# Stick-breaking scores as three products of high and low parts, with the low parts in two alternating sets of tiles

## The chip, the cores and the metric

The program runs on one core of a Trainium2 chip. The metric is the device time of one launch in microseconds. The kernel before took 2168.89 us (median of 3 runs, 2168.69 to 2169.61). In the profiles TensorE is PE (its weight loads PEld), VectorE is DVE, ScalarE is ACT, GpSimd is POOL and SyncE is SP.

## The reference, cut to what matters

A long chain of transformer blocks on 512 tokens of width 1024, float32 throughout. The part that the change touches is the stick-breaking attention, 16 heads of width 64:

```
qkv = (h @ w_qkv).reshape(b, s, 3, 16, 64)
z = einsum('bqhd,bshd->bhqs', q_blk, k) * 64**-0.5
causal = key_pos[None, :] < t[:, None]
log_1m = where(causal, log_sigmoid(-z), 0.0)
excl = cumsum(log_1m, axis=3, reverse=True) - log_1m
a = where(causal, exp(log_sigmoid(z) + excl), 0.0)
o = einsum('bhqs,bshd->bqhd', a, v)
```

A later block has another attention (two kinds of key sets, names nk_ks and nk_kw); it is not changed, but its scores are made in the way that the change brings to the stick-breaking ones.

## The kernel before

All activations lie transposed: features on the 128 partitions, the 512 tokens along the free axis. Large products are made from split operands: a high part rounded to fp32r and a low part (the rest), as hi*hi, hi*lo and lo*hi. ScalarE makes a high part (`act_hi`, `act_weights`), VectorE the low part from it (`dve_lo`, `dve_weights`), and TensorE takes three products of one pass each.

The stick-breaking stage (`pe_stick`, `act_stick`, `dve_stick`, `pool_stick`) works on head pairs c = 0 to 7: the two heads of a pair lie on partitions 0 to 63 and 64 to 127, and a pair's queries and keys are column blocks c of the tiles `q_s` and `k_s` (in the trace st_q and st_k). A pair takes four steps, n = 4c to 4c+3, for key blocks j = 3, 2, 1, 0, and the causal mask leaves 128, 256, 384 and 512 queries to them. In step n each engine works through its own written order, tied to the others by semaphores:

- TensorE: scores(n) into two PSUM banks (one per head), closed by a mask product of bf16 tiles (maskb, Ib); then the cumulative sums of step n-2 (`pe_stick_cum`, trir times high and low parts Lh, Ll); then half of a projection of queries or keys of the next pair (`pe_stick_qk`, 12 products of 512 columns); then the output product of step n-3 (`pe_stick_out`).
- VectorE: in every other step the low part of a weight unit (wl, L517) or, in the odd steps, the scaling of the finished projection out of PSUM into `q_s` (step 4c+1, L2615) or `k_s` (step 4c+3, L2617); then abs(n) (L2564), lo(n-1) (L2580), terms(n) (L2572), which waits for ScalarE's logarithm, and for two steps of four a low part of a sum (L2593). In steps 4c+2 it also splits a finished output (so_x, L571).
- ScalarE: the weights of step n-2 (exponential, L2515), in odd steps the high part of a weight unit (wh, L507), then exp(n) (L2530) and ln(n) (L2534); in steps 4 to 11 also the scaling of a block of the residual H (L2540).
- GpSimd: the high part of step n (L2689), sums of columns over key blocks (L2604, L2606, L2608), and in steps 4 to 11 the product of a block of H with rs1 (L2697).

The first two projections (pair 0) are made before the value projections, and the last head pair's keys are projected in steps 25 and 26; from step 27 on TensorE has no projection to fill a step with. Buffers are handed over by `plan` (who uses a buffer, and which marks free it) and `take` (waits for those marks). `NB` is the one PSUM bank in which projections land.

Of the kernel before, what the change touches and what calls it, by code (L numbers as in the profile page):

```python
# [4 lines left out]
F = mybir.dt.float32  # L5
# [201 lines left out]
def program(nc, A, cols_d, const_d, out_d):  # L207
# [85 lines left out]
    def plan(buf, ev, *freed):  # L293

        assert ev not in use, ev
        use[ev] = (buf.t, buf.freed)
        buf.freed = list(freed)
# [7 lines left out]
    def got(ev):  # L305
        return use[ev][0]
# [236 lines left out]
    def mm(e, out, a, b, start, stop):  # L543
        return e.matmul(out, a, b, start=start, stop=stop, skip_group_check=True)  # L544
# [68 lines left out]
    def plan_spread(n):  # L613
        plan(NB, ("spread", n), (a_made, ("rs", n)))
        plan(tmp.next(), ("diag", n), (mixed, ("spread", n)))
# [1661 lines left out]


    ph = Phase(XAT, "st")
    q_s = ph.sb("q", [128, 8, S])  # L2280
    k_s = ph.sb("k", [128, 8, S])
    XO = Pair(*(Phase(XAT + 4 * 8 * S * i, f"so{i}").sb("x", [128, 8, S], R) for i in range(2)))
    ph = Phase(PH0 + 32768, "st")
    v_s = ph.sb("v", [128, 4, D])
    rs1 = Phase(PH0 + 92160, "st").sb("rs1", [128, S])
    wd = [512 - 128 * j for j in range(4)]
    wl_ = [512, 384, 384, 128]
    ST = [(c, j) for c in range(8) for j in (3, 2, 1, 0)]
# [35 lines left out]
    OUT_LAST = [(2, 0, 3), (0, 7, 8), (1, 7, 8), (2, 3, 8)]  # L2324

    def plan_stick():
        for o in QK[0:2]:
            plan(psr.next(), ("sqk", o), (v_made, ("sqk", o)))
        for blk in range(2):
            token_plan(f"sv{blk}", 4)  # L2330
            if blk == 0:
                plan_spread("st")
        plan_spread("one")
        pairs = Ring([0, 1, 2])
        for n in range(-1, NST):
            u, half = next_qk(n)
            if u is not None and half == 0:
                plan(NB, ("sqk", QK[u]), (v_made, ("sqk", QK[u])))
            if n < 0:
                continue  # L2340
            c, j = ST[n]
            at = pairs.next()
            for m in range(2):
                plan(PS[2 * at + m], ("sk", n, m), (a_made, ("sw", n, m)))
            plan(Lp.next(), ("L", n), (mixed, ("so", n)))
            reader = [(scored, ("cum", n + 1 if j else n))]
            if j >= 2:
                reader.append((g_made, ("sum", n + 1)))
            plan(Lh[j].next(), ("Lh", n), *reader)
            plan(Ll[j].next(), ("Ll", n), *reader)  # L2350
            if j == 2:
                plan(sum2, ("sum", n), (v_made, ("lo_sum", n)))
            if j == 1:
                plan(sum1, ("sum", n), (v_made, ("lo_sum", n)))
                plan(later, ("later", n), (scored, ("cum", n + 1)))
            if j == 3:
                plan(PS[6], ("so", c), (x_lo, ("so", c)))
        for o, b in enumerate([NB, PS[4], PS[5], PS[0], PS[1], PS[2], PS[3], PS[6]]):
            plan(b, ("soo", o), (h_new, ("st", o)))
        plan_next("m")  # L2360
# [36 lines left out]
    def pe_stick_scores(e, n):  # L2397

        c, j = ST[n]
        e.wait_ge(*v_made.at("sqk", c))  # L2400
        e.wait_ge(*v_made.at("sqk", 8 + c))
        bk = [take(e, ("sk", n, m))[:, 0:wd[j]] for m in range(2)]
        for m in range(2):
            p0 = 64 * m
            mm(e, bk[m], k_s[p0:p0 + 64, c, 128 * j:128 * j + 128], q_s[p0:p0 + 64, c, 128 * j:512], True, False)
        for m in range(2):
            mm(e, bk[m][:, 0:128], Ib[:, :], maskb[:, 2, :], False, False).then_inc(*scored.up("z", n, m))

# [53 lines left out]
    def pe_stick(e):  # L2462
# [21 lines left out]
            project(e, f"so{o}", XO, "so", t[:, :], ("soo", o))  # L2484
        pe_.end("st")

    def act_stick(e):
        act_weights(e, UI["sv02"])
        fence(e, "f")
# [7 lines left out]
        for blk in range(2):  # L2497
            for c in range(4):
                act_weights(e, UI[f"sv{blk}{c}"] + 2)
                if blk == 0 and c == 2:  # L2500
                    act_rs(e, "st", [(v_made, ("f", ff.last_up))])
            if blk == 0:
                e.wait_ge(*v_made.at("inv", "st"))
            act_tokens(e, f"sv{blk}", lambda t: v_s[:, t, 512 * blk:512 * blk + 512], 512, 4, inv("st"))
# [12 lines left out]
        for n in range(-1, NST + 3):  # L2517
            if 2 <= n < NST + 2:
                weights_of(n - 2)
            u, half = next_qk(n)  # L2520
            if u is not None and half == 0:
                act_weights(e, UI[f"sq{QK[u]}"] + 2)
            if n == NST - 2:
                act_weights(e, UI["so2"])
            if 0 <= n < NST:
                c, j = ST[n]
                L = got(("L", n))
                for part in parts(n):
                    e.wait_ge(*v_made.at("abs", n, heads_of(part)[-1]))
                    e.activation(L[:, part, 0:wd[j]], L[:, part, 0:wd[j]], ACT.Exp, scale=-1.0).then_inc(  # L2530
                        *a_made.up("exp", n, part.start))
                for part in parts(n):
                    e.wait_ge(*a_made.at("exp", n, part.start))
                    e.activation(L[:, part, 0:wd[j]], L[:, part, 0:wd[j]], ACT.Ln, bias=ONE1).then_inc(  # L2534
                        *a_made.up("ln", n, part.start))
            if 4 <= n < 12:
                k = n - 4
                e.wait_ge(*h_new.at("f5", k))
                e.wait_ge(*x_lo.at("st", k))
                e.activation(H[:, k, :], H[:, k, :], ACT.Copy, scale=col("first", k)).then_inc(*a_made.up("first", k))  # L2540
            if n >= 6 and n % 4 == 2:
                c = n // 4 - 1
                e.wait_ge(*mixed.at("so", 4 * c + 3))
                act_hi(e, XO, "so", c, got(("so", c))[:, :])
# [63 lines left out]
        e.tensor_scalar(sum_parts(n)[0], f[:, :, :], 1.0, 0.0, ALU.mult, ALU.add).then_inc(*g_made.up("hi_sum", n))  # L2608

    def dve_stick_qk(e, o):  # L2610
        b, t = o % 8, got(("sqk", o))
        e.wait_ge(*proj.at("sqk", o))
        e.wait_ge(*a_made.at("rs", "st"))
        if o < 8:
            f = e.scalar_tensor_tensor(q_s[:, b, :], t[:, :], 0.125, rs[:, :], ALU.mult, ALU.mult)  # L2615
        else:
            f = e.tensor_tensor(k_s[:, b, :], t[:, :], rs[:, :], ALU.mult)  # L2617
        f.then_inc(*v_made.up("sqk", o))

    def dve_stick(e):  # L2620
        dve_weights(e, UI["sv02"])
# [13 lines left out]
        for blk in range(2):  # L2635
            for c in range(4):
                dve_weights(e, UI[f"sv{blk}{c}"] + 2)
                if blk == 0 and c == 2:
                    for o in QK[0:2]:
                        dve_stick_qk(e, o)  # L2640
        dve_diag(e, "one")
        for n in range(-1, NST + 3):
            u, half = next_qk(n)
# [7 lines left out]
                dve_stick_abs(e, n)  # L2651
            if 1 <= n < NST + 1:
                dve_stick_lo(e, n - 1)
            if 0 <= n < NST:
                dve_stick_terms(e, n)
            if 1 <= n < NST + 1 and ST[n - 1][1] in (1, 2):
# [963 lines left out]
```

## Time and profile before

| | |
|---|---|
| profiled execution, its own time | 2170.64 us |
| its span | 2168.8 us |
| median of 3 runs | 2168.89 us |
| PE busy | 2133.5 us (98%) |
| DVE, ACT, POOL busy | 71%, 46%, 34% |
| chain that ended last | PE 90%, DVE 4%, ACT 3% |
| stick-breaking steps, about | 906 to 1080 us of the span |

The profile is of one execution, somewhat longer than the median of the runs; a sum of changes is made against it and carried over to the median as a difference. A row's mean duration includes the time that an instruction is held up inside its engine, and on TensorE successive products overlap, so that what a group of products takes is read from start to start.

### The profile page before, as it was taken

To read this page: it belongs to the slowest core of one execution; us is meant where nothing else is said; L and a number is where in the kernel's file an instruction comes from. 1 tells how busy PE (TensorE), PEld (TensorE's weight loads), DVE (VectorE), ACT (ScalarE), POOL (GpSimd) and SP (SyncE) were. 2 spreads that over 40 slices of the span, in tenths; PEclk is the share of its full clock that TensorE was granted. 3 is DMA by queue.
4 is the path that set the end of the run, shared out by engine and by line. 5 is a ranking of instruction groups with operands and counts; after the bars stand their busy time and mean duration, and the time that the engine had idled before them with its cause. 6 is when DMAs were issued, how large, how long until landed. Compare 5 with 4: busy or idle time off the path is not lost.

```text
span 2168.8 us, 32272 instructions
## 1 busy us (share of the span) xinstructions
PE 2133.5 (98%) x12632; PEld 1776.1 (82%) x12632; DVE 1533.2 (71%) x2130; ACT 1003.7 (46%) x1690; POOL 728.4 (34%) x604
## 2 busy tenths in 40 slices
PE   8999999999999999999999999999989999999998
PEld 7888788888999998766688998988865568898987
DVE  5866566558988886386668777765567756877774
ACT  4433464445544444365554343344426755333434
POOL 2301330017434434164464232310136636332321
PEclk9999999999999999999999999999999999999999
DMA  5233125223333333311133323323410012323231
GB/s 177 83 107 88 50 78 170 74 59 88 98 117 98 117 96 89 88 49 49 30 88 99 116 88 107 115 80 123 121 49 2 1 38 80 117 82 114 89 106 49
DMA packets 292679, 188.06 MB, mean 87 GB/s; under 512 B 7856, under 2 KB 286768, under 8 KB 292528
## 3 DMA queue, kind: packets, MB, share of 16 engines
q1 hardware_dynamic: 292240, 185.78, 28.5%
q8 instruction: 101, 1.65, 0.3%
q14 instruction: 50, 0.41, 0.1%
q10 hardware_dynamic: 288, 0.21, 0.0%
HBM read 183.88 MB, written 2.10 MB: 86 GB/s over the span
## 4 chain that ended last, share of the span: by engine, by line
PE 90%; DVE 4%; ACT 3%; issue 2%; POOL 0%; DMA 0%; ACTq 0%; DVEq 0%; POOLq 0%
PE ps L544 88%; PE ps L578 2%; ACT wh L507 1%; DVE wl L517 1%; DVE H L687 0%; DVE tmp L1174 0%; ACT sq L621 0%; DVE tt_t L1921 0%; DMA p_xt<-in_x 0%; DVE sb_small L3228 0%; ACT tp_tb L1899 0%; DVE tp_up L2178 0%; ACT xb_x L565 0%; POOL acc L631 0%; DVE st_Ll L2580 0%
## 5 line engine op out<-in xcount | busy, mean ns | idle before, releaser
L517 DVE TENSOR_TENSOR wl<-raw,wh 128x1024 fp32r<-128x1024 f32 (+1 forms) x336 | 433.2, 1302 | 251.5 <-ACT wh L507 251.0
L544 PE MATMUL ps<-xb_x,wh 128*128 128x256 f32 (+1 forms) x1584 | 389.7, 337 | 1.9 <-DVE wl L517 0.7
L507 ACT CAST wh<-raw 128x1024 fp32r<-128x1024 f32 (+1 forms) x336 | 324.3, 980 | 137.6 <-PE ps L544 128.9
L544 PEld LDWEIGHTS ps<-xb_x,wh 128*128 128x128 f32 x1584 | 266.0, 188 | 32.6 <-issue 1.1
L544 PE MATMUL ps<-tt_t,wh 128*128 128x256 f32 x1536 | 277.8, 280 | 2.7 <-ACT tp_q L2105 2.6
L544 PE MATMUL ps<-xb_x,wl 128*128 128x256 f32 (+1 forms) x792 | 265.0, 335 | 0.0
L544 PEld LDWEIGHTS ps<-tt_t,wh 128*128 128x128 f32 x1536 | 237.5, 188 | 6.6 <-ACT tp_q L2105 3.6
L544 PE MATMUL ps<-XH,wh 128*128 128x512 f32 (+2 forms) x632 | 234.5, 371 | 4.3 <-issue 3.4
L544 PE MATMUL ps<-XH,wl 128*128 128x512 f32 (+2 forms) x632 | 229.6, 363 | 0.0
L544 PE MATMUL ps<-XL,wh 128*128 128x512 f32 (+2 forms) x632 | 229.3, 363 | 0.0
L544 PE MATMUL ps<-tt_t,wl 128*128 128x256 f32 x768 | 214.6, 279 | 0.0
L631 POOL TENSOR_TENSOR acc<-acc,sq 128x512 f32<-128x512 f32 x55 | 79.4, 1444 | 397.0 <-ACT sq L621 396.2
L529 POOL TENSOR_TENSOR su_s<-raw 128x512 f32<-128x512 f32 x48 | 65.1, 1356 | 397.3 <-DVE wl L517 376.6
L517 DVE TENSOR_TENSOR wl<-su_s,wh 128x1024 fp32r<-128x1024 f32 x96 | 124.1, 1293 | 57.1 <-ACT wh L507 56.7
L544 PEld LDWEIGHTS ps<-xb_x,wl 128*128 128x128 f32 x792 | 149.2, 188 | 16.3
L687 DVE TENSOR_TENSOR H<-H,ps 128x512 f32<-128x512 f32 x200 | 135.2, 679 | 23.6 <-PE ps L544 23.5
L544 PEld LDWEIGHTS ps<-tt_t,wl 128*128 128x128 f32 x768 | 144.7, 188 | 0.0
L544 PEld LDWEIGHTS ps<-XH,wh 128*128 128x128 f32 (+1 forms) x632 | 119.4, 189 | 24.8 <-issue 4.5
L544 PEld LDWEIGHTS ps<-XH,wl 128*128 128x128 f32 (+1 forms) x632 | 119.3, 189 | 19.5
L544 PEld LDWEIGHTS ps<-XL,wh 128*128 128x128 f32 (+1 forms) x632 | 119.5, 189 | 18.6 <-issue 0.7
L507 ACT CAST wh<-su_s 128x1024 fp32r<-128x1024 f32 x96 | 100.5, 1047 | 19.0 <-PE ps L544 16.6
L538 POOL TENSOR_TENSOR su_s<-raw,raw 128x512 f32<-128x512 f32 x48 | 70.3, 1464 | 103.8 <-DVE wl L517 103.8
(427 smaller groups left out, 4695.1 us busy)
## 6 DMA issues: line engine op xcount, KB each, us to landing
raw<-in_mlp_w SPq DMA_DIRECT2D x128, 512.0 KB, 4.0
raw<-in_w_gate_up SPq DMA_DIRECT2D x44, 512.0 KB, 4.0
raw<-in_w_in SPq DMA_DIRECT2D x29, 512.0 KB, 3.6
raw<-in_sb_w_qkv SPq DMA_DIRECT2D x24, 512.0 KB, 3.7
raw<-in_w_down SPq DMA_DIRECT2D x22, 512.0 KB, 5.9
raw<-in_w_out_mix SPq DMA_DIRECT2D x16, 512.0 KB, 3.7
raw<-in_w_kv SPq DMA_DIRECT2D x16, 512.0 KB, 4.0
raw<-in_nsa_w_kv SPq DMA_DIRECT2D x12, 512.0 KB, 3.7
```

Of the source, the lines that this page charges most:

```text
L507: e.copy(shaped(WH[i % NH], i), source(i)).then_inc(*w_hi.up(i))
L517: e.tensor_tensor(shaped(WL[i % NH], i), source(i), shaped(WH[i % NH], i).bitcast(F), ALU.subtract).then_inc(*w_lo.up(i))
L529: e.tensor_tensor(SU[0][:, 0:4, :], tb[:, 0::2, :], tb[:, 1::2, :], ALU.add).then_inc(*g_made.up())
L538: e.tensor_tensor(SU[1][:, 4:8, :], ta[:, 0::2, :], tb[:, 0::2, :], ALU.subtract).then_inc(*g_made.up())
L544: return e.matmul(out, a, b, start=start, stop=stop, skip_group_check=True)
L578: f = e.transpose(out[0:p, o:o + src.shape[0]], src, ident)
L631: e.tensor_tensor(a[:, :], a[:, :], got(("sq", n, k))[:, :], ALU.add).then_inc(*g_made.up("acc", n, k))
L687: e.tensor_tensor(H[:, o, :], H[:, o, :], src, ALU.add).then_inc(*h_new.up(ver, o))
```

## The change

Queries and keys of a head pair are no longer multiplied as float32 but as split operands. VectorE's scaling of a projection now writes a float32 tile (`tmp.bufs[2]` for queries, `tmp.bufs[3]` for keys); ScalarE rounds it into `q_s` or `k_s`, now fp32r (`act_stick_qk`); VectorE subtracts and writes the low part (`dve_stick_qk_lo`) into one of two sets of tiles, taken in turn by the pair's parity. The scores are k_hi*q_hi, k_hi*q_lo and k_lo*q_hi, each for both heads. The new waits: the first score product of a pair waits for the low parts of its queries and keys (`x_lo`), where it waited for the scaling; the low part waits for the high part; a float32 tile is free again when its low part is made, and a set of low tiles when the last scores of the pair two earlier are made.

```
+    q_s = ph.sb("q", [128, 8, S], R)
+    k_s = ph.sb("k", [128, 8, S], R)
...
+    phl = Phase(PH0 + 94208, "sl")
+    qk_lo = [[Phase(PH0 + 90112, "sl").sb("a", [128, S], R), phl.sb("b", [128, S], R)],
+             [phl.sb(f"c{i}", [128, S], R) for i in range(2)]]
+    qk_low = [[Buf(t) for t in pair] for pair in qk_lo]
...
+        def plan_parts(u):
+            o = QK[u]
+            plan(tmp.bufs[2 + u % 2], ("qkt", o), (x_lo, ("qk", o)))
+            plan(qk_low[o % 8 % 2][o // 8], ("qkl", o), (scored, ("z", 4 * (o % 8) + 3, 1)))
...
     def pe_stick_scores(e, n):
         c, j = ST[n]
-        e.wait_ge(*v_made.at("sqk", c))
-        e.wait_ge(*v_made.at("sqk", 8 + c))
+        e.wait_ge(*x_lo.at("qk", c))
+        e.wait_ge(*x_lo.at("qk", 8 + c))
         bk = [take(e, ("sk", n, m))[:, 0:wd[j]] for m in range(2)]
-        for m in range(2):
-            p0 = 64 * m
-            mm(e, bk[m], k_s[p0:p0 + 64, c, 128 * j:128 * j + 128], q_s[p0:p0 + 64, c, 128 * j:512], True, False)
+        ql, kl = got(("qkl", c)), got(("qkl", 8 + c))
+        for k, q, first in ((k_s[:, c, :], q_s[:, c, :], True), (k_s[:, c, :], ql, False),
+                            (kl, q_s[:, c, :], False)):
+            for m in range(2):
+                p = slice(64 * m, 64 * m + 64)
+                mm(e, bk[m], k[p, 128 * j:128 * j + 128], q[p, 128 * j:512], first, False)
...
+    def act_stick_qk(e, o):
+        e.wait_ge(*v_made.at("sqk", o))
+        e.copy((k_s if o >= 8 else q_s)[:, o % 8, :], got(("qkt", o))[:, :]).then_inc(*x_hi.up("qk", o))
...
     def act_stick(e):
+                if blk == 0 and c == 3:
+                    for o in QK[0:2]:
+                        act_stick_qk(e, o)
...
+            if half == 0 and 2 < (n + 1) // 2 + 2 <= 16:
+                act_stick_qk(e, QK[(n + 1) // 2 + 1])
             if 0 <= n < NST:
...
     def dve_stick_qk(e, o):
-            f = e.scalar_tensor_tensor(q_s[:, b, :], t[:, :], 0.125, rs[:, :], ALU.mult, ALU.mult)
+            f = e.scalar_tensor_tensor(d[:, :], t[:, :], 0.125, rs[:, :], ALU.mult, ALU.mult)
...
+    def dve_stick_qk_lo(e, o):
+        d, hi = take(e, ("qkl", o)), (k_s if o >= 8 else q_s)[:, o % 8, :]
+        e.wait_ge(*x_hi.at("qk", o))
+        e.tensor_tensor(d[:, :], got(("qkt", o))[:, :], hi.bitcast(F), ALU.subtract).then_inc(*x_lo.up("qk", o))
...
     def dve_stick(e):
+                if blk == 1 and c == 0:
+                    for o in QK[0:2]:
+                        dve_stick_qk_lo(e, o)
...
             if 1 <= n < NST + 1:
                 dve_stick_lo(e, n - 1)
+            if half == 0 and 2 < (n + 1) // 2 + 2 <= 16:
+                dve_stick_qk_lo(e, QK[(n + 1) // 2 + 1])
             if 0 <= n < NST:
                 dve_stick_terms(e, n)
```

Where the instructions stand now, on VectorE in the last step of a head pair (n = 4c+3). Names: so_x is the output of the pair before, st_L the work tile of a step, st_Lh and st_Ll its high and low part; tmp_78 is the new float32 tile of the keys, sl_b their low part. Line numbers are those of each kernel. Before:

```order
L571 TENSOR_TENSOR so_x<-ps,so_x 128x512
L2617 TENSOR_TENSOR st_k<-ps,rs 128x512
L2564 TENSOR_SCALAR st_L_144<-ps 128x512 x2
L2580 TENSOR_TENSOR st_Ll_151<-st_L_143,st_Lh_146 128x384 x2
L2572 SCALAR_TENSOR_TENSOR st_L_144<-ps,st_L_144 128x512 x2
L2593 TENSOR_TENSOR sr_l<-sr_f_157,sr_h 128x512
L517 TENSOR_TENSOR wl_66<-raw_56,wh_62 128x1024
```

Now:

```order
L571 TENSOR_TENSOR so_x<-ps,so_x 128x512
L2645 TENSOR_TENSOR tmp_78<-ps,rs 128x512
L2592 TENSOR_SCALAR st_L_148<-ps 128x512 x2
L2608 TENSOR_TENSOR st_Ll_155<-st_L_147,st_Lh_150 128x384 x2
L2651 TENSOR_TENSOR sl_b<-tmp_78,st_k 128x512
L2600 SCALAR_TENSOR_TENSOR st_L_148<-ps,st_L_148 128x512 x2
L2621 TENSOR_TENSOR sr_l<-sr_f_161,sr_h 128x512
L517 TENSOR_TENSOR wl_66<-raw_56,wh_62 128x1024
```

The low part of the keys stands behind abs and both halves of lo(n-1), and ahead of terms(n).

On ScalarE in the same step, with the waits of each instruction. Before:

```order
L563 CAST so_x<-ps 128x512 [waits mixed]
L2515 ACTIVATE st_L_142<-ps 128x256 [waits scored,pool_made]
L2515 ACTIVATE st_L_142<-ps 128x256 [waits scored]
L507 CAST wh_64<-raw_59 128x1024 [waits projected,weights_in_3]
L2530 ACTIVATE st_L_144<-st_L_144 128x512 [waits dve_made] x2
L2534 ACTIVATE st_L_144<-st_L_144,small 128x512 [waits act_made] x2
```

Now:

```order
L563 CAST so_x<-ps 128x512 [waits mixed]
L2541 ACTIVATE st_L_146<-ps 128x256 [waits scored,pool_made]
L2541 ACTIVATE st_L_146<-ps 128x256 [waits scored]
L507 CAST wh_64<-raw_59 128x1024 [waits projected,weights_in_3]
L2508 CAST st_k<-tmp_78 128x512 [waits dve_made]
L2558 ACTIVATE st_L_148<-st_L_148 128x512 [waits dve_made] x2
L2562 ACTIVATE st_L_148<-st_L_148,small 128x512 [waits act_made] x2
```

The rounding of the keys stands between the weight unit and exp(n); in step 4c+1 that of the queries stands at the same place.

On TensorE where the next pair begins, before:

```order
L544 MATMUL ps<-st_L_141,st_v 64x128 x2
L544 MATMUL ps<-st_q,st_k 128x128 [waits act_made]
L544 MATMUL ps<-st_q,st_k 128x128
L544 MATMUL ps<-maskb,Ib 128x128 x2
L544 MATMUL ps<-st_Lh_146,trir 128x384 [waits dve_made]
```

Now (sl_c_143 and sl_c_144 are the low parts of that pair's queries and keys):

```order
L544 MATMUL ps<-st_L_145,st_v 64x128 x2
L544 MATMUL ps<-st_q,st_k 128x128 [waits act_made,x_lo]
L544 MATMUL ps<-st_q,st_k 128x128
L544 MATMUL ps<-sl_c_143,st_k 128x128 x2
L544 MATMUL ps<-st_q,sl_c_144 128x128 x2
L544 MATMUL ps<-maskb,Ib 128x128 x2
L544 MATMUL ps<-st_Lh_150,trir 128x384 [waits dve_made]
```

The first product of the pair now waits for x_lo, and the two float32 products have become six.

## Rows read from the trace of the kernel before

**Rows 1.** Page of the profile, part 4: shares of the chain that ended last, by engine
```profile
PE 90%; DVE 4%; ACT 3%; issue 2%; POOL 0%; DMA 0%; ACTq 0%; DVEq 0%; POOLq 0%
```

**Rows 2.** Busy time by stretch: stretch, its length, each engine's busy us (instructions), PEclk, DMA share, GB/s
```profile
945.60:967.85 22.25, 22.25 (x122) 15.23 (x120) 18.76 (x30) 14.72 (x28) 16.48 (x17) 1.00 0.16 48
```

**Rows 3.** Timeline of TensorE, scores today: start us, us, engine, line, operation, tiles, count
```profile
967.85 0.49 PE L544 MATMUL ps<-st_q,st_k 64*128 64x128 f32 x4
973.06 0.70 PE L544 MATMUL ps<-st_q,st_k 64*128 64x256 f32 x4
979.37 0.92 PE L544 MATMUL ps<-st_q,st_k 64*128 64x384 f32 x4
984.71 1.13 PE L544 MATMUL ps<-st_q,st_k 64*128 64x512 f32 x4
985.77 0.28 PE L544 MATMUL ps<-maskb,Ib 128*128 128x128 bf16 x2
```

**Rows 4.** Timeline of TensorE, scores of the later attention, made as three products
```profile
1662.71 0.50 PE L544 MATMUL ps<-nk_kwh,xb_x 64*128 64x512 f32 x2
1663.61 0.29 PE L544 MATMUL ps<-maskb,Ib 128*128 128x128 bf16 x2
1665.72 0.45 PE L544 MATMUL ps<-nk_kwh,xb_x 64*128 64x384 f32 x2
1666.44 0.28 PE L544 MATMUL ps<-maskb,Ib 128*128 128x128 bf16 x2
1668.11 0.39 PE L544 MATMUL ps<-nk_kwh,xb_x 64*128 64x256 f32 x2
1668.67 0.29 PE L544 MATMUL ps<-maskb,Ib 128*128 128x128 bf16 x2
1669.91 0.33 PE L544 MATMUL ps<-nk_kwh,xb_x 64*128 64x128 f32 x2
1670.39 0.29 PE L544 MATMUL ps<-maskb,Ib 128*128 128x128 bf16 x2
```

**Rows 5.** Timeline of VectorE around the change to head pair 3
```profile
963.18 0.69 DVE L571 TENSOR_TENSOR so_x<-ps,so_x 128x512 fp32r<-128x512 f32 x1 [0.42 <-ACT so_x L563]
965.58 2.00 DVE L2580 TENSOR_TENSOR st_Ll<-st_L,st_Lh 128x384 fp32r<-128x384 f32 x2
967.77 1.30 DVE L2572 SCALAR_TENSOR_TENSOR st_L<-ps,st_L 128x512 f32<-128x512 f32 x2 [0.19 <-ACT st_L L2534]
```

**Rows 6.** Timeline of GpSimd, same stretch
```profile
964.97 1.30 POOL L2606 TENSOR_TENSOR sr_f<-sr_f,st_Ll 128x512 f32<-128x512 f32 x1
966.36 0.82 POOL L2608 TENSOR_SCALAR sr_h<-sr_f 128x512 fp32r<-128x512 f32 x1
967.14 1.58 POOL L2697 TENSOR_TENSOR H<-H,st_rs 128x512 f32<-128x512 f32 x1
```

**Rows 7.** Timeline of VectorE, the other head pairs and the end
```profile
920.48 2.22 DVE L2580 TENSOR_TENSOR st_Ll<-st_L,st_Lh 128x384 fp32r<-128x384 f32 x2
978.77 0.76 DVE L2572 SCALAR_TENSOR_TENSOR st_L<-ps,st_L 128x256 f32<-128x256 f32 x2 [3.06 <-ACT st_L L2534]
987.84 1.02 DVE L2580 TENSOR_TENSOR st_Ll<-st_L,st_Lh 128x384 fp32r<-128x384 f32 x2
1054.59 1.02 DVE L2580 TENSOR_TENSOR st_Ll<-st_L,st_Lh 128x384 fp32r<-128x384 f32 x2
1055.99 1.30 DVE L2572 SCALAR_TENSOR_TENSOR st_L<-ps,st_L 128x512 f32<-128x512 f32 x2 [0.38 <-ACT st_L L2534]
```

**Rows 8.** Timeline of ScalarE, same change as rows 5
```profile
965.03 1.04 ACT L507 CAST wh<-raw 128x1024 fp32r<-128x1024 f32 x1
```

**Rows 9.** Groups by line and form, ScalarE: busy us, mean ns, idle before
```profile
L563 ACT CAST fm_h<-tp_up 128x512 fp32r<-128x512 f32 x32 | 19.9, 621 | 111.4 <-DVE tp_up L2178 111.4
```

**Rows 10.** Timeline of TensorE at the end of the stage
```profile
1054.28 0.49 PE L544 MATMUL ps<-st_q,st_k 64*128 64x128 f32 x4 [0.20 <-ACT st_L L2515]
1058.99 0.50 PE L544 MATMUL ps<-st_Lh,trir 128*128 128x512 f32 x1 [0.60 <-DVE st_Ll L2580]
```

More of the change, by code:

```diff
@@ L2279, in program @@
     ph = Phase(XAT, "st")
-    q_s = ph.sb("q", [128, 8, S])
-    k_s = ph.sb("k", [128, 8, S])
+    q_s = ph.sb("q", [128, 8, S], R)
+    k_s = ph.sb("k", [128, 8, S], R)
     XO = Pair(*(Phase(XAT + 4 * 8 * S * i, f"so{i}").sb("x", [128, 8, S], R) for i in range(2)))
@@ L2326, in plan_stick, with plan_qk @@
     def plan_stick():
+        def plan_qk(o, bank):
+            plan(bank, ("sqk", o), (v_made, ("sqk", o)))
+        def plan_parts(u):
+            o = QK[u]
+            plan(tmp.bufs[2 + u % 2], ("qkt", o), (x_lo, ("qk", o)))
+            plan(qk_low[o % 8 % 2][o // 8], ("qkl", o), (scored, ("z", 4 * (o % 8) + 3, 1)))
         for o in QK[0:2]:
-            plan(psr.next(), ("sqk", o), (v_made, ("sqk", o)))
+            plan_qk(o, psr.next())
         for blk in range(2):
@@ L2332, in plan_stick @@
                 plan_spread("st")
+        for u in range(2):
+            plan_parts(u)
         plan_spread("one")
+        for u in range(2, 16):
+            plan_parts(u)
         pairs = Ring([0, 1, 2])
@@ L2337, in plan_stick @@
             if u is not None and half == 0:
-                plan(NB, ("sqk", QK[u]), (v_made, ("sqk", QK[u])))
+                plan_qk(QK[u], NB)
             if n < 0:
@@ L2610, in dve_stick_qk @@
     def dve_stick_qk(e, o):
-        b, t = o % 8, got(("sqk", o))
+        d, t = take(e, ("qkt", o)), got(("sqk", o))
         e.wait_ge(*proj.at("sqk", o))
@@ L2614, in dve_stick_qk @@
         if o < 8:
-            f = e.scalar_tensor_tensor(q_s[:, b, :], t[:, :], 0.125, rs[:, :], ALU.mult, ALU.mult)
+            f = e.scalar_tensor_tensor(d[:, :], t[:, :], 0.125, rs[:, :], ALU.mult, ALU.mult)
         else:
-            f = e.tensor_tensor(k_s[:, b, :], t[:, :], rs[:, :], ALU.mult)
+            f = e.tensor_tensor(d[:, :], t[:, :], rs[:, :], ALU.mult)
         f.then_inc(*v_made.up("sqk", o))
+    def dve_stick_qk_lo(e, o):
+        d, hi = take(e, ("qkl", o)), (k_s if o >= 8 else q_s)[:, o % 8, :]
+        e.wait_ge(*x_hi.at("qk", o))
+        e.tensor_tensor(d[:, :], got(("qkt", o))[:, :], hi.bitcast(F), ALU.subtract).then_inc(*x_lo.up("qk", o))
     def dve_stick(e):
```

## The prediction

> **What bounds the kernel now.** The page of the profile comes first: the chain that ended last is PE for 90% [rows 1]. A change in one stage has to be read from that stage, so next the busy time by stretch: a head pair of the stick-breaking stage takes 22.25 us, in which PE is busy for all 22.25, DVE for 18.8, ACT for 14.7, POOL for 16.5, at full clock [rows 2]. The scores of pairs 1 to 6 start at 923.36, 945.60, 967.85, 990.10, 1012.35 and 1034.60, one period apart (945.60 and 967.85 are the ends of rows 2): nothing makes PE wait there. What PE saves there counts one for one, if DVE and ACT, which get more to do, deliver in time. In the last pair PE does wait (two waits are in rows 10), and there VectorE and ScalarE set the pace.
>
> **What PE gains.** The scores of one step now take, from their first product to the next group, 0.43, 0.63, 0.85 and 1.06 us for 128, 256, 384 and 512 queries. Rows 3 show 1.06 for the widest (984.71 to 985.77); the row says 1.13, so a row overlaps the next by 0.07, and the others, 0.49, 0.70 and 0.92, give 0.42, 0.63 and 0.85. Sum of a pair: 2.96 us. The new form is in the trace already, in the later attention: three products of high and low parts, two heads on 64 partitions each, the same weights' width, the same kind of products ahead and the same mask behind [rows 4]. There the group takes 1663.61-1662.71 = 0.90, 0.72, 0.56 and 0.48, sum 2.66. The gain is 0.16, 0.13 and 0.07 for the wide ones and a loss of 0.06 for the narrowest, 0.30 us a pair. The two heads run side by side there: six times 512 columns one after the other, a column a cycle at the full clock of 2.4 GHz, would be 1.28 us, and the group takes 0.90. So the gain is small from the start: 8 x 0.30 = 2.4 us at most.
>
> **What is added beside it.** Sixteen roundings on ACT and sixteen subtractions on DVE. A rounding of 128x512 from a float32 tile takes 0.62 us [rows 9]; successive instructions overlap a little, and I take 0.55 as the shift of what follows. A subtraction of 128x512 I take at 0.68: two of 128x384 take 1.02 when undisturbed (at 987.84 in [rows 7]), 0.51 each, times 4/3. The pair 0 ones lie in the value projections, where PE has only large products; no product waits for them (uncovered they would cost 0.55 + 0.68 each). The queries' subtraction (step 4c+1) lies before terms(n), where DVE waits 3.06 us for ACT (at 978.77) [rows 7]: hidden; without that idle time it would push DVE back by 0.68. The queries' rounding delays exp, ln and terms of step 4c+1 by 0.55, and with them GpSimd, which from there works without a gap to the end of the next two steps. Instruction counts on PE grow by 4 products a step; their time is in the 0.90.
>
> **The keys' subtraction is not hidden.** It stands in step 4c+3 behind lo(n-1), and PE's next group of scores waits for it; behind that group PE's queue holds the sums of step n-1, half a projection and an output product, and ACT and DVE wait for the first two. So the question is when lo(n-1) ends and when PE comes. Work it out for the change to pair 3. PE comes at 967.85 [rows 3], or, since the products of the two steps after the last common point (PE's output product, which so_x waits for) shrink by 0.13 and 0.16, at 967.56. lo ends at 965.58+2.00 = 967.58 [rows 5]. Already with the bare 0.68 behind it the low part would be 0.7 us late.
> It gets later, for DVE and POOL hinder each other. The two halves of lo take 2.00 us here and 1.02 at 987.84. The first starts at 965.58 while POOL's L2606 runs till 966.27; then POOL's L2608 shows 0.82 us and ends at 967.18, and DVE's second half ends 0.40 after that; then POOL's L2697, issued at 967.14, ends 1.14 after DVE is done [rows 5, 6]. The rows read as strict turns between DVE instructions with two SBUF inputs and POOL's. With turns: POOL comes 0.55 later by the queries' rounding, so L2606 ends at 966.8, DVE's first half at 967.25, L2608 at 967.7, the second half at 968.1, and L2697, which has been waiting longer than the keys' subtraction, at 969.3; the subtraction behind it ends at 969.85. PE starts 2.3 us late. The Trainium skill, page "SBUF — State Buffer", section "Summary: rules for kernel authors", says that where DVE has two SBUF inputs and GpSimd reads SBUF, the second to issue "fully blocks until the first finishes". By that rule the wait is the 2.3 us; if the two only slowed each other, so that the subtraction ran from 967.6 at the doubled 1.0 us, it would be about 1.0.
> L2697 exists in steps 4 to 11 only, so the 2.3 us fall due twice, at the changes to pairs 2 and 3: 4.6 us.
> Change to pair 1 (923.36): lo is 920.48+2.22 = 922.70 [rows 7], with no L2697 behind it; the subtraction ends at 923.35, PE comes at 923.05 (three wide groups and a narrow one saved 0.30): wait 0.3.
> Changes to pairs 4, 5, 6: lo ends at 988.86, one turn later with POOL's shift 989.1, the subtraction 989.75; PE comes at 990.10-0.29 = 989.81. Wait 0, and with little to spare; bounds 0 and 0.4 each.
> Change to pair 7: PE has no projection in step 27 and comes at 1054.28 [rows 10], the subtraction ends behind lo (1054.59+1.02 = 1055.61 [rows 7]) at about 1056.4, 2.1 us later, but here DVE and ACT set the pace and PE has idle time of its own. The rounding pushes terms(27) from 1055.99 [rows 7] to about 1056.4, and PE, with scores, sums and scores in front of it, reaches the sums of step 27 perhaps 0.6 later than 1058.99 [rows 10]; one group's gain of 0.1 goes off. I take +0.5; the bounds are 0 and the whole 2.1.
> ACT's shift of 0.55 in step 4c+3 lies beside DVE's: ACT's weight cast ends at 966.07 [rows 8], the rounding at 966.6, so the high part is there before lo ends. terms(n), now at 967.77 [rows 5], follow the subtraction, but PE needs them only in its sums of step n+2, six us later, and is itself late by then.
>
> **The sum.** Gain 0.30-0.31 for six pairs that are bounded by PE: -1.8 to -1.9. Waits: 0.3 + 4.6 + 0. End: +0.5. Net +3.5 us. Against the profiled execution's own time, 2170.64 us (span 2168.8 and 1.8 around it), this is 2174.1; against the median of the runs, 2168.89, which stands 1.75 lower, 2172.4. That is 0.16%. About 0.2%, or 4.3 us, is what a measurement of this kernel can tell from no change.
>
> **The rivals.**
> A, DVE keeps up: the low parts never stop PE, because so_x and all behind it on DVE follow PE's faster steps or POOL lets DVE through. 2168.9-2.4 = 2166.5. For it speaks only DVE's idle share; against it that lo ends at 967.58 when PE wants to start at 967.56. Chance 0.08.
> B, contention without turns: the subtraction passes ahead of L2697; waits of 1.0 to 1.25 at two changes: net +1.0 to +1.4, 2170.1. Chance 0.22.
> C, the slower one: every one of the seven changes makes PE wait, because the place of the keys' subtraction has no room at the changes to pairs 4 to 6 either (0.06 us spare by my sum), and at those with L2697 a further POOL instruction gets in between. It decides from 0.1 us more on DVE or POOL. Three waits of 0.4 and 0.7 more at each of the two: 3.5+1.2+1.4 = +6.1, 2175.0. Chance 0.23.
> D, the products don't behave as in the later attention: the bounds are the two heads one after the other (3 x 1280 more columns a pair, 1.6 us, 13 us in all, 2185) and no overhead beside the columns (1.0 us a pair off, 8 us in all, 2164). Nothing in the rows speaks for either: chance 0.04, half each side.
> The forecast has 0.43.
>
> **How the numbers follow.** Forecast 2172.4, its own range 2171.2 to 2173.6. The range leaves out A and D and most of C's upper end: 2168.6 to 2175.6. Faster by over 0.2% (under 2164.6) is left to D's lucky half and to what I don't see: 0.04. Slower by over 0.2% (over 2173.2) are C, D's other half and the upper edge of the forecast, 0.23+0.02+0.05: 0.30. Within: 0.66.
>
> **What the changed profile would show.** Score groups of 0.48, 0.56, 0.72 and 0.90 us start to start. PE idle just ahead of the first scores of a pair, released by DVE's subtraction (tile sl): about 2.3 us at pairs 2 and 3, 0.3 at pair 1, none or little at 4 to 6, about 2 at 7. At pairs 2 and 3 the subtraction should show 1.8 us, ending right after POOL's L2697 plus 0.6. Periods of 24.2 us for the pairs with L2697 and 21.95 for the later ones. I am wrong in the mechanism if PE never waits on sl, or waits alike everywhere; wrong in size if the subtraction overtakes L2697; wrong in the place if the time sits outside 900 to 1080 us.

## The result, and the profile after

| kernel | median us (lowest to highest, runs) | to the kernel before |
|---|---|---|
| before | 2168.81 (2168.69 to 2169.61, 4) | |
| changed | 2176.99 (2176.27 to 2178.76, 4) | 1.0038 [1.0026, 1.0050] |

The change costs 8.2 us, 0.38%. I had said 2172.4, 2168.6 to 2175.6: slower than I had it, and outside the range. A second measurement of the same kernel (`after2`) gave 2177.87, 1.0041 [1.0029, 1.0054]. The profiled execution of the changed kernel took 2178.76 (span 2176.6), the slowest of its four; the profiled execution of `after2` is the median one of its five (2177.87, span 2175.8), and sums are made with it.

The chain is still TensorE's, with a little more of VectorE in it. Page of the changed kernel, part 4 (answers to [rows 1]):

```profile
PE 89%; DVE 5%; ACT 3%; issue 2%; POOL 0%; DMA 0%; ACTq 0%; DVEq 0%; POOLq 0%
```

Busy time by stretch, changed kernel: a head pair with GpSimd's product of H in it, and a later one (columns as in [rows 2]):

```profile
945.68:971.46 25.78, 23.83 (x128) 17.21 (x128) 21.04 (x32) 15.86 (x29) 16.47 (x16) 0.93 0.15 41
993.59:1015.73 22.14, 22.14 (x130) 15.86 (x129) 17.40 (x31) 13.43 (x26) 10.27 (x12) 1.00 0.16 48
```

Before, both took 22.25. The later pair is only 0.11 shorter, although the scores in it are 0.30 shorter; the earlier one is 3.5 longer, and two things show in its row: PE is idle for 1.95 of it, and its granted clock is 0.93.

What PE waits for in the stage, 900 to 1095 us, without the one wait at its start (0.7 us for st_rs) that both kernels have (engine, tile, line waited for: us in total, times, longest). Changed kernel:

```profile
PE ps L544 <- DVE sl_c L2651: 4.8, 3, 2.8
PE ps L544 <- DVE sl_b L2651: 1.9, 1, 1.9
PE ps L544 <- DVE st_Ll L2608: 1.8, 2, 1.1
```

Kernel before:

```profile
PE ps L544 <- DVE st_Ll L2580: 2.3, 4, 0.9
PE ps L544 <- ACT st_L L2515: 0.5, 2, 0.3
```

The subtraction (L2651) is the new releaser, 6.7 us of it; each of these waits stands at the first scores of a pair. Timeline of TensorE in the changed kernel, those first scores (pairs 1, 2, 3, 5, 7) and the widest group of pair 4:

```profile
921.49 0.33 PE L544 MATMUL ps<-st_q,st_k 64*128 64x128 f32 x2 [0.16 <-DVE sl_c L2651]
945.68 0.33 PE L544 MATMUL ps<-st_q,st_k 64*128 64x128 f32 x2 [1.90 <-DVE sl_b L2651]
971.46 0.33 PE L544 MATMUL ps<-st_q,st_k 64*128 64x128 f32 x2 [1.85 <-DVE sl_c L2651]
1010.30 0.50 PE L544 MATMUL ps<-st_q,st_k 64*128 64x512 f32 x2
1011.19 0.29 PE L544 MATMUL ps<-maskb,Ib 128*128 128x128 bf16 x2
1015.73 0.33 PE L544 MATMUL ps<-st_q,st_k 64*128 64x128 f32 x2
1059.82 0.47 PE L544 MATMUL ps<-st_q,st_k 64*128 64x128 f32 x2 [2.76 <-DVE sl_c L2651]
```

The widest group takes 1011.19-1010.30 = 0.89, the narrowest 0.48, the others 0.55 and 0.73, as in [rows 4] within 0.01. Note 0.47 at 1059.82 where the same row says 0.33 elsewhere.

Around the change to pair 3 (answers to [rows 5] and [rows 6]), VectorE and then GpSimd:

```profile
967.25 2.49 DVE L2608 TENSOR_TENSOR st_Ll<-st_L,st_Lh 128x384 fp32r<-128x384 f32 x2
969.66 1.75 DVE L2651 TENSOR_TENSOR sl_c<-tmp,st_k 128x512 fp32r<-128x512 f32 x1
971.33 1.27 DVE L2600 SCALAR_TENSOR_TENSOR st_L<-ps,st_L 128x512 f32<-128x512 f32 x2
```

```profile
968.52 0.81 POOL L2636 TENSOR_SCALAR sr_h<-sr_f 128x512 fp32r<-128x512 f32 x1
969.30 1.56 POOL L2735 TENSOR_TENSOR H<-H,st_rs 128x512 f32<-128x512 f32 x1
```

The subtraction is issued at 969.66, the product of H (issued before it, at 969.30) ends at 970.86, the subtraction 0.55 after that, and PE starts at 971.46. At pair 5, with no product of H, it runs undisturbed:

```profile
1013.43 1.43 DVE L2608 TENSOR_TENSOR st_Ll<-st_L,st_Lh 128x384 fp32r<-128x384 f32 x2
1014.78 0.68 DVE L2651 TENSOR_TENSOR sl_c<-tmp,st_k 128x512 fp32r<-128x512 f32 x1
```

1.75 against 0.68: the turns are there. The rule I had weighed (the Trainium skill, "SBUF — State Buffer", "Summary: rules for kernel authors") fits this.

The clock is what I had left out. Busy time by stretch, changed kernel, behind the waits of pairs 2, 3 and 7 (the third column from the right is the granted clock of TensorE):

```profile
947.00:950.00 3.00, 3.00 (x11) 2.61 (x10) 3.00 (x5) 1.49 (x4) 3.00 (x2) 0.50 0.00 0
974.00:978.00 4.00, 4.00 (x26) 2.75 (x24) 4.00 (x8) 0.93 (x2) 2.36 (x2) 1.00 0.44 131
1060.00:1066.00 6.00, 6.00 (x30) 4.58 (x31) 4.09 (x11) 1.79 (x4) 2.04 (x3) 0.50 0.00 0
```

TensorE had been idle for 1.90 us ahead of the first, 1.85 ahead of the second and 2.76 ahead of the third, and after the first and third it works at the lower of its two levels, 1.2 GHz instead of 2.4, on the products that everything waits for. In `after2` pair 2 is at full clock (1.00 over 947 to 950 us), and pair 7 is at half for most of the stretch (0.55 over 1060 to 1066). In the kernel before no stretch of the stage is below 1.00.

**The sum, read off two profiles** (before and `after2`; first scores of a step to first scores of another). The first scores of step 27, the last of pair 6, and of step 31, the last of the stage, are these, in the kernel before:

```profile
1051.45 1.13 PE L544 MATMUL ps<-st_q,st_k 64*128 64x512 f32 x4
1065.82 1.13 PE L544 MATMUL ps<-st_q,st_k 64*128 64x512 f32 x4
```

and in `after2`:

```profile
1053.58 0.50 PE L544 MATMUL ps<-st_q,st_k 64*128 64x512 f32 x2
1071.56 0.50 PE L544 MATMUL ps<-st_q,st_k 64*128 64x512 f32 x2
```

From pair 0 to the last step of pair 6 145.11 us became 148.53, +3.42. From there to the last scores of the stage 14.37 became 17.98, +3.61. From those scores to the end 1103.02 became 1104.21, +1.19; in 1600 to 1660 us, which the change doesn't touch, the granted clock is 0.94 in the one and 0.89 in the other. Together +8.22. (The spans differ by 6.9 only, since the profile of before has half clock near 540 us, 0.91 over 530 to 550 us where `after2` has 1.00, and with it reaches the stage at 906.34 instead of 905.05.)

### The profile page after: what moved, and what is told of

It is laid out like the page before. It is cut to its first block, busy times and chain, and to the rows that moved or that the text cites. A ratio compares the mean times of both kernels' runs of the same rounds, so it can differ in the third digit from the quotient of the medians.

```text
span 2176.6 us, 32447 instructions
## 1 busy us (share of the span) xinstructions
PE 2135.2 (98%) x12696; PEld 1782.6 (82%) x12696; DVE 1549.2 (71%) x2146; ACT 1012.5 (47%) x1706; POOL 729.5 (34%) x604
## 4 chain that ended last, share of the span: by engine, by line
PE 89%; DVE 5%; ACT 3%; issue 2%; POOL 0%; DMA 0%; ACTq 0%; DVEq 0%; POOLq 0%
PE ps L544 87%; PE ps L578 2%; ACT wh L507 1%; DVE wl L517 1%; DVE st_Ll L2608 0%; DVE st_L L2592 0%; DVE H L687 0%; DVE tmp L1174 0%; ACT sq L621 0%; ACT XH L565 0%; ACT p_xscr L727 0%; DMA p_xt<-in_x 0%; ACT st_L L2558 0%; DVE st_L L2600 0%; ACT tp_tb L1899 0%
```

## The experiments

Twelve kernels in three groups (the first four rows, the next four, the last four), each group on a chip of its own with the kernel before beside it (2168.81, 2168.95 and 2169.35); across groups the ratios are what to compare. T is the theory of the prediction, that the low parts come late through their place and through the turns with GpSimd; the expectations add to it the half clock behind the waits, which the prediction did not have.

| kernel | median us | ratio [interval] |
|---|---|---|
| `after2`, the changed kernel | 2177.87 | 1.0041 [1.0029, 1.0054] |
| `load` | 2171.71 | 1.0012 [1.0003, 1.0021] |
| `nolow` | 2169.05 | 1.0000 [0.9992, 1.0009] |
| `filler` | 2174.42 | 1.0025 [1.0015, 1.0034] |
| `fe` | 2171.56 | 1.0011 [1.0002, 1.0020] |
| `early` | 2171.86 | 1.0012 [1.0003, 1.0021] |
| `early_fe` | 2169.34 | 1.0001 [0.9993, 1.0010] |
| `before_fe` (control) | 2170.27 | 1.0003 [0.9994, 1.0012] |
| `nb` | 2174.33 | 1.0025 [1.0014, 1.0037] |
| `best` | 2167.79 | 0.9992 [0.9984, 1.0001] |
| `best_nofe` | 2168.50 | 0.9997 [0.9988, 1.0006] |
| `before_nb` (control) | 2169.59 | 0.9999 [0.9991, 1.0008] |

**after2.** No edit.

> The changed kernel as it is, once more, as the measure for the others. Theory T: the 8 us are (1) the wait of TensorE for the keys' low part at the seven changes of head pair, about 6 us in sum, and (2) TensorE running at half its clock after the waits of 1.9 us and more (change to pairs 2, 3 or 7), about 1.6 us after pair 2 and some 3 us around pair 7, less (3) the gain of some 2 us in the products. Then this run lies at 2176.3 to 2178.8 again, and where a long wait is not followed by half clock it lies lower. Rival L (load): the sixteen roundings and subtractions slow the stage by themselves, wherever they stand. Rival P (products): the three products cost more than they save.

Measured 2177.87 (2176.03 to 2180.27). Its profile has the waits at the same places; the half clock at pair 2 is missing. The mean granted clock of an execution goes with its time: 0.991 at 2180.27, 0.992 at 2177.87, 0.994 at 2176.03. So the scatter between executions is at least partly the clock's.

**load: the added instructions alone.** The kernel before, with roundings and subtractions made into spare tiles that nobody reads.

```
+        e.copy(xh_[u % 2][:, :], (k_s if o >= 8 else q_s)[:, o % 8, :]).then_inc(*x_hi.up("qk", o))
...
+        e.tensor_tensor(xl_[u % 2][:, :], (k_s if o >= 8 else q_s)[:, o % 8, :], xh_[u % 2][:, :].bitcast(F), ALU.subtract).then_inc(*x_lo.up("qk", o))
```

> The kernel before with the change's roundings and subtractions added at the change's places, but with scores still float32 and TensorE not waiting for the low parts (they are made and not used). T: TensorE idles nowhere before pair 7, nothing falls to half clock; 2168.8 to 2170.2 (+0 to +1.4, all of it in the last pair). L: this kernel bears the same load, so it is as slow as the changed one or slower: 2175 or more.

2171.71, between the two. What PE waits for on VectorE in `load`, and of its two longest waits the one in pair 2:

```profile
PE ps L544 <- DVE st_Ll L2595: 4.4, 6, 0.9
```

```profile
951.42 0.51 PE L544 MATMUL ps<-st_Lh,trir 128*128 128x512 f32 x1 [0.95 <-DVE st_Ll L2595]
```

Nobody waits for the spare tile, but it still costs 2.9 us: VectorE, held back by the subtraction in step 7 (1.78 us beside GpSimd), delivers lo(7) late for the sums of that step, which PE makes in step 9, and the same again four steps on, in the two pairs with GpSimd's product of H (1.17 and 1.13 us more from the scores of step 4c+1 to the next). The other 0.6 lies in the last pair. In the changed kernel this does not come on top: PE has already lost more than that at the first scores, and the same step takes 6.20 to 6.23 us there, undisturbed. So neither theory's number came out. The load has a price of its own, and in the changed kernel it is contained in the wait ahead of it.

**nolow: everything but the subtraction.** All pairs use the low parts of pair 0 in place of their own (so the scores of pairs 1 to 7 are not the reference's); 14 subtractions are gone, the products and roundings stay, and the first scores of a pair wait for the rounding instead.

```
-        ql, kl = got(("qkl", c)), got(("qkl", 8 + c))
+        ql, kl = got(("qkl", 0)), got(("qkl", 8))
...
-            if half == 0 and 2 < (n + 1) // 2 + 2 <= 16:
-                dve_stick_qk_lo(e, QK[(n + 1) // 2 + 1])
```

> The changed kernel without the fourteen subtractions of pairs 1 to 7: all pairs use the low parts of pair 0, so the output is not the reference's; roundings and six products a step stay. T: periods of a head pair 22.25-0.30 = 21.95 us, no idle time at the changes, 2166.5 to 2168 (1 to 2.4 us under the kernel before). P: no faster than the kernel before, periods of 22.25 or more. L: about 2173, half of the loss, since the roundings are still there.

2169.05: the subtractions and their waits are 8.8 us of the changed kernel, as T has it. But 2 us of gain should have been left over, and nothing is. P had foreseen that time, but for another reason: the score groups are as short as T has them. Still, at the changes to pairs 2 to 6 the time from the scores of step 4c+3 to the next ones is 5.40 to 5.56, as long as before or longer. That was a new question (see `nb`).

**filler: the clock alone.** Eight products of 512 columns, into the bank that the scores then overwrite, ahead of PE's wait at pairs 2, 3 and 7. The low parts come as late as before; PE only isn't idle meanwhile.

```
+        bk = [take(e, ("sk", n, m))[:, 0:wd[j]] for m in range(2)]
+        if j == 3 and c in (2, 3, 7):
+            for _ in range(8):
+                mm(e, got(("sk", n, 0))[:, :], trir[:, 0, :], XB.hi[:, 0, :], True, True)
         e.wait_ge(*x_lo.at("qk", c))
         e.wait_ge(*x_lo.at("qk", 8 + c))
-        bk = [take(e, ("sk", n, m))[:, 0:wd[j]] for m in range(2)]
```

> The changed kernel with eight products of 512 columns (about 1.85 us), written to a score bank and overwritten, put ahead of TensorE's wait at the changes to pairs 2, 3 and 7. T: they fit into the waits of 1.9 to 2.8 us, the clock stays at full there, and the kernel gets faster by what half clock cost, 1.6 us at pair 2 and up to 3 at pair 7: 2172.5 to 2175. If half clock is not the cause of those times, the kernel stays at 2177 or gains the fillers' time, up to +5.5 us.

2174.42, 3.45 less than `after2` on the same chip, with more work. The first scores of pair 7 come as late as in the changed kernel (5.24 us behind those of step 27, 5.22 in `after2`), but behind them there is no half clock:

```profile
1060.00:1066.00 6.00, 5.91 (x44) 4.05 (x43) 3.55 (x11) 4.29 (x9) 1.03 (x2) 1.00 0.00 0
```

and from the scores of step 27 to those of step 31 it takes 15.24 us instead of 17.98:

```profile
1053.13 0.51 PE L544 MATMUL ps<-st_q,st_k 64*128 64x512 f32 x2
1068.37 0.50 PE L544 MATMUL ps<-st_q,st_k 64*128 64x512 f32 x2
```

So the clock costs 2.74 us at pair 7, and the wait with all that follows from it 15.24-14.37 = 0.87.

**fe: no product of H beside the keys' subtraction.** GpSimd's eight products, one each in steps 4 to 11, and ScalarE's scaling ahead of each go to steps 4, 8, 12 and 16, two each.

```
+    FE = {4: (0, 1), 8: (2, 3), 12: (4, 5), 16: (6, 7)}
-            if 4 <= n < 12:
-                k = n - 4
+            for k in FE.get(n, ()):
```

> The changed kernel, with GpSimd's product of a block of H with rs1 (and ScalarE's scaling ahead of it) moved from steps 4 to 11, one in each, to steps 4, 8, 12 and 16, two in each: none is left in a step 4c+3 at pairs 2 and 3. T (the waits at pairs 2 and 3 are GpSimd's product going ahead of the keys' subtraction, in turns): both waits of 1.9 us fall to 0.2 or less, with them the half clock that can follow them, 4 to 5 us less than the changed kernel's 2177: 2171.5 to 2173. What is left over the kernel before is pair 7 and what lies behind it. Rival U (the subtraction comes late because VectorE itself has too much in step 4c+3, and GpSimd only happens to run then): the waits stay at 1 us or more each, 2175 to 2177.

2171.56: of the 9.1 us that `after2` is over its kernel before, 2.6 are left. Timeline of VectorE and of TensorE at the change to pair 2 in `fe`:

```profile
942.82 0.68 DVE L2651 TENSOR_TENSOR sl_b<-tmp,st_k 128x512 fp32r<-128x512 f32 x1
```

```profile
943.74 0.33 PE L544 MATMUL ps<-st_q,st_k 64*128 64x128 f32 x2
```

1.75 has become 0.68, the wait of 1.90 is gone, at pair 3 too. Both are thus the turns with GpSimd, and U is out. Pair 7, which has no product of H, still waits 2.76, and the profiled execution (2173.36) has half clock behind it. The eleven executions spread from 2169.34, at a mean granted clock of 0.996, to 2173.61, at 0.992. The profiles of `load`, `nolow` and `filler`, with full clock throughout the stage, show 0.996 too, so the fastest execution of `fe` probably had no half clock at pair 7; no profile shows it.

**early: the place of the subtraction.** Rounding ahead of ScalarE's weight unit, subtraction ahead of lo(n-1). The part on VectorE:

```
+            if half == 0 and 2 < (n + 1) // 2 + 2 <= 16:
+                dve_stick_qk_lo(e, QK[(n + 1) // 2 + 1])
             if 1 <= n < NST + 1:
                 dve_stick_lo(e, n - 1)
-            if half == 0 and 2 < (n + 1) // 2 + 2 <= 16:
-                dve_stick_qk_lo(e, QK[(n + 1) // 2 + 1])
```

> The changed kernel with the keys' and queries' rounding ahead of ScalarE's weight unit, and the subtraction ahead of lo(n-1) on VectorE. T (what costs is the place of the subtraction behind lo): the low part is there when PE comes, waits on it fall to 0.4 or less at pairs 2 and 3 and from 2.8 to about 1.4 at pair 7, no half clock at pair 7; lo comes 0.7 later, so some of it turns into waits on st_Ll, in the steps with GpSimd's product above all. 2169 to 2171.5. Rival V (the added instructions cost the same wherever they stand, as in the kernel with unused low parts, +2.9 us, plus pair 7): 2173 or more, the waits moved to st_Ll.

2171.86, just over T's range. The only wait on the low parts left is 1.41 at pair 7. But lo, behind it, now meets the turns:

```profile
PE ps L544 <- DVE st_Ll L2608: 3.1, 5, 1.1
PE ps L544 <- DVE sl_c L2651: 1.4, 1, 1.4
```

At pairs 2 and 3 the time from the scores of step 4c to those of 4c+1 is 0.85 us more than undisturbed (6.12 and 6.09 against 5.26), and the next another 0.37. V is right in this much: with GpSimd's product beside it, the load makes something late at either of these two places (a third one, in `best_nofe`, costs less).

**early_fe: both.**

> Both moves in one kernel. T: no wait on the low parts at pairs 1 to 6, the gain of the products (0.3 a pair at pair 0 to 1, 0.1 a pair as measured at 4 to 6) is left, pair 7 costs 1 us or less: 2167 to 2169, at or below the kernel before. Rival V: 2171 or more.

2169.34: level with the kernel before, 0.3 over the range I had given, well under V's. There is no wait on a low part before pair 7, where 1.41 is left.

**before_fe: control.** The move of `fe` on the kernel before.

> Control: the kernel before with only the same move of GpSimd's product of H. T: TensorE never waited for it at the changes of pairs there, so within 0.05% of the kernel before, 2168 to 2169.5. If this move alone gains more than 1 us, the comparison of the changed kernel with it has to be read against this one.

1.0003 [0.9994, 1.0012]: the move alone gains nothing; the median is 0.8 over my range, within what the interval allows.

**nb: where the gain of the later pairs went.** The changed kernel, with VectorE's scaling of the keys put ahead of so_x (which waits for ScalarE):

```
+            if 7 <= n < 28 and n % 4 == 3:
+                c = n // 4 - 1
+                dve_lo(e, XO, "so", c, got(("so", c))[:, :])
             if 0 <= n < NST:
                 dve_stick_abs(e, n)
...
-            if n >= 6 and n % 4 == 2:
+            if n >= 30 and n % 4 == 2:
```

> The changed kernel with one swap on VectorE in the steps 4c+3 of pairs 1 to 6: the scaling of the keys' projection out of PSUM goes ahead of the low part of the finished output (so_x), which waits for ScalarE. W (the second half of a projection has one PSUM bank, free when the scaling has read it; the faster scores bring TensorE to the next projection 0.16 us earlier, the scaling stays where it was behind so_x, and the gain turns into a wait for the bank): from the scores of step 4c+3 to those of step 4c+4 now 5.40 to 5.44 us at pairs 4 to 6, becomes 5.25, and the projection's first product follows the sums by 0.11 us instead of 0.26. That is worth 0.5 to 0.8 us in all, 2175.5 to 2177; the waits on the keys' low part stay. Rival X (the 0.16 is lost in the products themselves, whatever stands ahead): 5.40 stays.

Timeline of TensorE where the sums end and the projection begins: changed kernel,

```profile
1012.12 0.27 PE L544 MATMUL ps<-st_Ll,trir 128*128 128x128 f32 x1
1012.38 0.49 PE L544 MATMUL ps<-xb_x,wh 128*128 128x512 f32 x1
```

and the scaling on VectorE that frees the projections' only PSUM bank there:

```profile
1011.64 0.68 DVE L2645 TENSOR_TENSOR tmp<-ps,rs 128x512 f32<-128x512 f32 x1
```

In `nb`:

```profile
1017.09 0.27 PE L544 MATMUL ps<-st_Ll,trir 128*128 128x128 f32 x1
1017.20 0.68 PE L544 MATMUL ps<-xb_x,wh 128*128 128x512 f32 x2
```

The projection starts 0.26 behind the last sum in the one, 60 ns after the scaling's end (1012.32), and 0.11 in the other; from scores to scores 5.41 to 5.44 becomes 5.21 at pairs 4, 5 and 6. W is right, X wrong. Of the time the run says less: five executions between 2173.87 and 2174.43, two at 2181.7. The profiled one is one of these two, and shows why: half clock behind three waits. Its stretches behind those of pairs 2 and 3:

```profile
947.00:950.00 3.00, 3.00 (x15) 2.88 (x14) 3.00 (x6) 0.51 (x2) 2.89 (x3) 0.50 0.00 0
974.00:979.00 5.00, 5.00 (x21) 4.45 (x20) 5.00 (x8) 1.79 (x4) 3.88 (x3) 0.50 0.15 37
```

There it is 8.20 and 8.26 us from the scores of step 4c to those of 4c+1 against 5.26, so 2.9 and 3.0 more, 5.9 of the 7.6 between the two levels. The mean granted clock is 0.990 in the two and 0.994 in the five. The lower level, 2174.0, is below the range I had given, more than the 0.6 us of W explain; which stretches of half clock those executions lacked no profile shows.

**best: all of it.** `early_fe` with the swap of `nb`, the subtraction ahead of abs(n) too, and the rounding ahead of the weights of step n-2:

```
+            u, half = next_qk(n)
+            if half == 0 and 2 < (n + 1) // 2 + 2 <= 16:
+                act_stick_qk(e, QK[(n + 1) // 2 + 1])
             if 2 <= n < NST + 2:
                 weights_of(n - 2)
```

> Everything that delivers the low parts early, in one kernel: GpSimd's products of H moved to steps 4, 8, 12 and 16; the scaling ahead of so_x; the subtraction ahead of abs(n) and lo(n-1) on VectorE, the rounding ahead of the weights of step n-2 on ScalarE. T with W: TensorE waits for no low part at pairs 1 to 6 and for 0.3 us at most at pair 7, from scores to scores 5.25 us at every change of pair, and the gain of 0.30 a pair is whole: 2 to 2.4 us under the kernel before, 2166.5 to 2167.2. Rival V (the added 2 x 8 instructions cost by themselves, through lo, exp and terms): waits on st_Ll come instead, 2169 or more.

2167.79 (2167.30 to 2168.72, 11 runs), 0.9992 [0.9984, 1.0001]. That is some 10 us under the changed kernel, and 1.6 under the kernel before by the medians, but the interval reaches 1: it is not shown to be faster. All that PE waits for in it between 918 and 1052 us (from the last step of pair 0 to pair 7):

```profile
PE ps L544 <- DVE tmp L2645: 0.3, 1, 0.3
PE ps L544 <- ACT st_L L2542: 0.2, 1, 0.2
```

Every later pair takes 21.92 to 21.93 us (22.24 to 22.26 before), pair 6 to pair 7 19.37 (19.67): 0.32 to 0.33 a pair, the whole gain of the products. At the first pair 0.30 is lost, again on the bank of the projections:

```profile
918.84 0.72 PE L544 MATMUL ps<-xb_x,wh 128*128 128x512 f32 x2 [0.30 <-DVE tmp L2645]
```

First scores to last take 157.91 us against 159.48, a gain of 1.57: six times 0.32 less 0.30 and less 0.07 in the last pair. The median is 0.6 over the range I had given.

**best_nofe: is the move of H's products needed then?**

> The same kernel with GpSimd's product of H left in steps 4 to 11. T: the keys' subtraction now is ahead of lo(n-1) and GpSimd, but lo and the sums behind it are later by its 0.68 us and take turns with GpSimd's product: two waits on st_Ll of about 1 us each at pairs 2 and 3 as in the kernel with both moved ahead of lo, 2168.5 to 2169.5, about 2 us over the version without them. Rival: the earlier place is enough by itself, then no difference, 2167.

2168.50. The step behind the first scores is undisturbed (5.26), the next one is 0.18 and 0.62 over 6.20 at pairs 2 and 3, in all 0.8 in the profile and 0.7 in the median, instead of the 2 I had expected: with the subtraction ahead of abs(n), lo keeps almost its old place.

**before_nb: control.** Both moves on the kernel before.

> Control: the kernel before with the same two moves (GpSimd's products of H to steps 4, 8, 12 and 16, and the scaling ahead of so_x). W: in it the projection finds its bank free, 0.11 us behind the sums, so nothing is gained: within 0.05% of the kernel before, 2168.2 to 2169.8. If it gains 1 us or more, the moves and not the products are what makes a rearranged version faster.

0.9999 [0.9991, 1.0008]: nothing. So the rearrangement is worth 10 us in the changed kernel and nothing in the old one.

## Why the prediction was wrong

**What held.** The groups (0.48, 0.55, 0.73, 0.89 measured, 0.48, 0.56, 0.72, 0.90 foreseen). The turns, and the two waits at pairs 2 and 3: PE came 2.27 and 2.24 us later than the shorter scores would have let it (7.50 and 7.48 from scores to scores against 5.39 and 5.40, less 0.16), foreseen 2.3; the subtraction 1.75, foreseen 1.8. The wait at pair 1 0.16, foreseen 0.3. None at pairs 4 to 6. Rivals A, B and C are out: the low parts do stop PE, the subtraction does not pass GpSimd (`fe` shows what it looks like alone), and three changes of pair have no wait. So is D, since the groups take what they take in the later attention.

**The step that failed: "Change to pair 7", "I take +0.5".** From the scores of step 27 to the last of the stage it was +3.61. I had looked for the whole price in what PE, DVE and ACT owe each other there, and that part was nearly right: `filler`, in which the low parts are as late but PE has something to do, measures 0.87. The other 2.74 us are the half clock that follows PE's 2.76 us of idle. The sum takes every duration behind a wait from rows at full clock; the same error lies in the two waits at pairs 2 and 3, which were priced as waits alone. There the clock took nothing in `after2`, 1.6 us in the profiled execution of the changed kernel, and 5.9 in that of `nb`. With +3.61 for the +0.5, the forecast would have been 2175.5, at the upper edge of the range.

**A second term, mis-sized: "Gain 0.30-0.31 for six pairs".** It was 0.11 to 0.14 at pairs 4 and 5 (22.14 and 22.15 us in the changed kernel, 22.12 in `after2`, 22.25 and 22.26 before). The shorter products save the rest too, but the projection behind them then waits for its bank, because the scaling is tied to so_x and so to ScalarE and to an output product of the step before, and does not come earlier when the scores do. My own wording was that what PE saves counts one for one "if DVE and ACT [...] deliver in time", and I checked this for the low parts only. From pair 0 to step 27 the sum was 3.05 and is 3.42; the 0.16 to 0.19 lost against the forecast at each of three pairs, some 0.5, is more than this difference. `nb` gives it back.

**A third, which the sum had at nothing.** It is the 1.19 us behind the stage. The stretch near 1630 us with half clock is there in every profile, before and after. Its size differs, and the time from the last scores to the end follows it:

```profile
1600.00:1660.00 60.00, 52.04 (x372) 32.35 (x370) 46.01 (x117) 29.57 (x92) 31.18 (x42) 0.94 0.04 11
1600.00:1660.00 60.00, 52.59 (x358) 33.47 (x357) 44.40 (x108) 25.08 (x78) 29.48 (x37) 0.89 0.07 18
```

The first row is the kernel before, the second `after2`. That time is 1102.8 to 1103.3 us in the eight profiles with 0.94, 1104.0 to 1104.3 in the five with 0.89 (the changed kernel, `after2`, `fe`, `nb` and the control `before_nb`), and 1103.0 in `early`, which has 0.91. So the 1.19 is this stretch's, and nothing else behind the stage got slower. What sets its size stays open. The changed kernel's instructions don't decide it, since `best` has the small one and `before_nb` the large one, and neither does the time within the span at which the program gets there by itself: the last scores start at 1063.99 in `early_fe`, with 0.94, and at 1064.00 in `before_nb`, with 0.89.

The range failed for the first reason: no case in it had PE slower after a wait. With that term right the forecast would have lain 1.5 us under the measured time, which the other two terms, 0.37 and 1.19, make up. The unknown that I bounded at pair 7 went from 0 to "the whole 2.1", as if the wait were the most that a wait can cost.

## What to carry to other kernels

A wait of some 2 us on a TensorE that was never idle can cost more than its length: look for what the products behind it would take at half clock, and put it into the range as a cost of the wait (here 2.7 us behind 2.8, none to 3.0 behind 1.9 to 2.2). When products on the critical path get shorter, follow each buffer that the next ones need back to what frees it; a chain through other engines that started before the saving does not move, and some 0.2 of 0.3 us a pair went there. And extra work on an engine with 15% of idle time costs according to its place: with the same sixteen roundings and subtractions the kernel is 8 us slower when they stand behind lo and beside GpSimd, and not measurably slower when they stand ahead of both.

## What was not expected of the hardware

Half clock came after idle times of 1.41 us (`early` and `early_fe`, granted clock 0.93 over 1050 to 1075 us) to 2.76, and did not come after 1.85 in the profiled execution of the changed kernel, nor after about 1.9 at pair 2 in `after2`: the same wait in the same kernel is followed by it or not. The Trainium skill, page "TensorE: Matmul & The Clock Gate", section "Part 1: The HAM clock gate (the "warmup" mystery)", calls the number of slow products at a kernel's start "run-variable"; here it is so in the middle of a kernel, and `nb` falls into two levels 7.6 us apart, at a mean granted clock of 0.990 and 0.994. Eight products that compute nothing, put ahead of each of three waits, took 3.45 us off the time.
